# Moving three normalisations off the hand-over between stages of a fused transformer kernel

## The reference, cut to what matters

```
x = x + merged @ w_out
x = x + conv_ffn(rmsnorm(x, ffn_norm_g), w_up, conv_w, conv_b, w_down)      # 22 chunks of 128 columns
x = rmsnorm(x, final_norm_g)                                                # block 1 ends
u_lat = rms_norm(x, norm_g) * (1 + sc_l) + sh_l                             # block 2, 1024 tokens
u_ctx = rms_norm(ctx, norm_g) * (1 + sc_c) + sh_c                           # 256 tokens of context
p_lat = u_lat @ mla_w_in      # query latent (256), key latent (128), rotary part (64), gate (1024)
p_ctx = u_ctx @ mla_w_in[:, kv]
```

## Time and profile before

| | before |
|---|---|
| median of 3 runs (lowest to highest) | 2555.14 us (2554.55 to 2556.97) |
| profiled execution, its own time | 2560.54 us |
| its span | 2558.7 us |
| its mean granted clock of PE | 0.986 |
| PE busy | 2468.8 us, 96% of the span |
| DVE busy | 1513.8 us, 59% |
| ACT busy | 868.5 us, 34% |
| POOL busy | 758.0 us, 30% |
| matmuls L733 (8 chunks of H or H2) | 1070.1 us, x4512 |
| matmuls L1032 (up) on BT, on B | 247.0 us, 190.7 us |
| matmuls L1061 (down) | 239.8 us |

### The profile page before, as it was taken

One profiled execution on the slowest core, in us unless ns is written; L12 is line 12 of the kernel. 1 busy time (PEld: TensorE's weight loads), 2 busy tenths in 40 slices (PEclk: granted clock), 3 DMA queues, 4 the chain that ended last, 5 costly groups with the idle time before them and its releaser, 6 DMA issues.

```text
span 2558.7 us, 33196 instructions
## 1 busy us (share of the span) xinstructions
PE 2468.8 (96%) x12060; PEld 2035.9 (80%) x12060; DVE 1513.8 (59%) x1981; ACT 868.5 (34%) x1290; POOL 758.0 (30%) x442
## 2 busy tenths in 40 slices
PE   7999999999999999999999979999999989899997
PEld 5777787787787888888888868788888878688886
DVE  7856674735557877777411663377777764633454
ACT  4232222223224544445100232156666651222121
POOL 3232232332333555555344412200000003222221
PEclk9999999999999999999999989999999999999999
DMA  5134243421422223233553211100000002111112
GB/s 181 42 115 140 99 149 108 140 74 50 164 107 107 99 107 123 98 113 133 222 194 135 77 41 33 58 1 17 8 8 8 9 9 62 32 40 33 41 41 74
DMA packets 54417, 210.70 MB, mean 82 GB/s; under 512 B 6420, under 2 KB 7700, under 8 KB 49082
## 3 DMA queue, kind: packets, MB, share of 16 engines
q1 hardware_dynamic: 50340, 194.92, 22.0%
q10 hardware_dynamic: 3990, 14.59, 1.6%
HBM read 173.30 MB, written 38.55 MB: 83 GB/s over the span
## 4 chain that ended last, share of the span: by engine, by line
PE 84%; DVE 9%; issue 4%; ACT 1%; DMA 1%; POOL 1%; DVEq 0%; SPq 0%; ACTq 0%; POOLq 0%
PE PS L733 39%; PE PS L1032 16%; PE PS L1061 9%; PE PS L1277 4%; PE PS L1210 3%; PE PS L1216 2%; PE PS L1249 2%; PE PS L891 1%; PE PS L926 1%; DVE cols L2777 1%; PE PS L1200 1%; DVE SC L2327 1%; PE PS L766 1%; PE PS L774 1%; PE PS L1427 1%
## 5 line engine op out<-in xcount | busy, mean ns | idle before, releaser
L733 PE MATMUL PS<-H,w_hl 128*128 128x512 f32 x4512 | 1070.1, 396 | 31.8 <-DVE H L2142 9.4
L733 PEld LDWEIGHTS PS<-H,w_hl 128*128 128x128 f32 x4512 | 847.6, 190 | 231.7 <-issue 33.5
L682 POOL CAST w_hl<-w_raw 128x1024 fp32r<-128x1024 f32 x138 | 155.1, 1124 | 1546.7 <-PE PS L733 1011.8
L684 POOL TENSOR_TENSOR w_hl<-w_raw,w_hl 128x1024 fp32r<-128x1024 f32 x138 | 348.2, 2523 | 11.0
L1032 PE MATMUL PS<-BT,WS 128*128 128x512 f32 x1056 | 247.0, 389 | 0.0
L1061 PE MATMUL PS<-FFD,w_hl 128*128 128x512 f32 x1056 | 239.8, 389 | 0.1
L1032 PEld LDWEIGHTS PS<-BT,WS 128*128 128x128 f32 x1056 | 198.2, 188 | 41.6 <-issue 0.5
L1061 PEld LDWEIGHTS PS<-FFD,w_hl 128*128 128x128 f32 x1056 | 198.1, 188 | 41.6 <-DVEq L2450 0.5
L1032 PE MATMUL PS<-B,WS 128*128 128x512 f32 x792 | 190.7, 395 | 3.6 <-issue 3.6
L1032 PEld LDWEIGHTS PS<-B,WS 128*128 128x128 f32 x792 | 151.1, 191 | 35.7 <-issue 4.0
L689 POOL TENSOR_TENSOR WS<-w_raw,WS 128x512 fp32r<-128x512 f32 x88 | 140.3, 1605 | 73.1 <-ACT WS L1745 72.8
(11 more groups left out here) (341 smaller groups left out, 3005.2 us busy)
## 6 DMA issues: line engine op xcount, KB each, us to landing
w_raw<-in_units SPq DMA_DIRECT2D x186, 512.0 KB, 3.6
AW<-in_ada SPq DMA_DIRECT2D x48, 512.0 KB, 4.2
ff_part<-FFS SPq DMA_DIRECT2D x20, 1024.0 KB, 4.9
FFD<-ff_part SPq DMA_DIRECT2D x20, 1024.0 KB, 5.6
X<-in_x SPq DMA_DIRECT2D x8, 512.0 KB, 8.7
x_part<-SC SPq DMA_DIRECT2D x8, 512.0 KB, 2.6
X<-x_part SPq DMA_DIRECT2D x4, 1024.0 KB, 8.7
out<-X SPq DMA_DIRECT2D x16, 256.0 KB, 2.1
```

What stands on the lines that cost most here:

```text
L682: pool.tensor_copy(hi_part, raw).then_inc(w_hi, 1)
L684: pool.tensor_tensor(lo_part, raw, hi_part.bitcast(F32), ALU.subtract).then_inc(w_split, 1)
L733: mm = pe.matmul(PS[:, out_at + a:out_at + a + m], w(s, wp, w0 + k), src[:, o:o + m], start=(k == 0 and wp == 0 and xp == 0), stop=(k == k ...
```

## The change

Four things change. (1) The query units `cq` run on X * gain, split during `down3` ("rows": ACT `row_hi`, DVE `row_lo`, after each chunk's squares) into H2; the norm's factor r (RS, a copy in SBUF) multiplies their results (`latent_rows`), and the shift enters through `shift_sum`, 16 one-column matmuls for each unit. PE begins `cq` straight after `down3`, with the norm's sum after four chunks, the spread after the first unit. H2 is then rewritten with factor and shift, as before, by `apply_split`, now while the second query unit runs, chunk behind chunk (`h_used`), and `kvpe` waits for it. (2) The context's norm moves forward: ACT loads and squares the context right after the up stage, DVE reduces it before `down0`'s first residual turn; PE sums it within `down0` and spreads it at its end; DVE and ACT write UC between the residuals of `down1` and `down2`. (3) Homes of spilled chunks are dealt anew, and two waits of SP move. (4) In the first up pair the norm's sum goes behind product 3 and its spread behind product 6; ACT takes the first two snapshots before `late_hi`, the weights' high parts 2 and 3 are written earlier, and DVE splits BT2, BT4 and BT3 before it turns to the factor.

```diff
     ("down0", {0: 4, 1: 4, "unit": 4, "xnew": 8}),
+    ("cnorm", {**NORM, "split": 8}),
     ("down1", {2: 4, 3: 4, "unit": 8, "xnew": 8}),
     ("down2", {2: 4, 3: 4, "unit": 8, "xnew": 8}),
-    ("down3", {2: 4, 3: 5, "unit": 8, "xnew": 9, "square": 18}),
-    ("norm3", {2: 2, 3: 1, "norm": 1, "split": 16}),
+    ("down3", {2: 4, 3: 5, "unit": 8, "xnew": 9, "square": 18, "split": 8}),
+    ("norm3", {**NORM, "split": 8}),
...
-    HOMES = [[2, 3, 0, 1], [4, 5, 6, 7, 8, 9], [10, 11, 12, 13, 14, 15], [0, 1, 2, 3, 4, 5]]
+    HOMES = [[2, 3, 0, 1], [4, 5, 8, 9, 10, 11], [6, 7, 0, 1, 2, 3], [8, 9, 10, 11, 14, 15]]
...
                 for half in range(2):
-                    sp.wait_ge(done[half], before("down1", half))
+                    sp.wait_ge(done[half], before("cnorm", half))
+        for half in range(2):
+            sp.wait_ge(done[2 + half], before("down2", 2 + half))
         for k in range(4):
             ff_load(3, k)
             load_until(d0 + 14 + k)
-        for half in range(2):
-            sp.wait_ge(done[2 + half], before("down2", 2 + half))
+        sp.wait_ge(lo, before("down3", "split"))
         for k in range(4, 6):
...
-                if first and n == 1:
+                if first and n == 3:
                     norm_sum(before("norm2", "norm"), before("norm2", 2), early=before("norm2", "square") - 1)
-                elif first and n == 3:
+                elif first and n == 6:
                     norm_spread(before("norm2", "norm"), before("norm2", 3))
...
                             opens = False
             return mm
 
+        def context_sum():
+
+            pe.wait_ge(st_free, 6 + 3 * FFC)
+            take(2, b("cnorm", 2))
+            pe.wait_ge(acc_ready, before("cnorm", "norm") + 1)
+            for j in range(CTX // P):
+                mm = pe.matmul(PS[:, 2048 + j:2049 + j], ACCX[:, j * P:(j + 1) * P], ones[:, 0:1], start=True, stop=True)
+            mm.then_inc(done[2], 1)
+
+        def context_spread():
+
...
         def first_down():
 
             u0 = before("down0", "unit")
@@ -1084,8 +1105,11 @@
                     down_unit(0, s, 1024, w0=ks, opens=False, k0=ks - 1).then_inc(done[1], 1)
                 else:
                     down_unit(0, s, 0).then_inc(done[0], 1)
+                    if i == 2:
+                        context_sum()
                     take(1, i + b("down0", 1))
                     down_unit(0, s, 1024, w0=ks, opens=False).then_inc(done[1], 1)
...
@@ -1113,25 +1137,33 @@
         for n in range(1, len(DOWN)):
             later_down(n)
 
-        norm_sum(before("norm3", "norm"), before("norm3", 2), ((ACC, T), (ACCX, CTX), (ACC2, T)),
-                 early=before("norm3", "square") - 2)
+        def shift_sum(j, s):
+
+            for k in range(KC):
+                for part in range(2):
+                    mm = pe.matmul(PS[:, 2560 - 512 * j:2561 - 512 * j], w(s, part, k).bitcast(F32), modb[:, k:k + 1],
+                                   start=(k == 0 and part == 0), stop=(k == KC - 1 and part == 1))
+            return mm
+
+        u, rows = before("cq", "unit"), before("down3", "split")
+        take(0, b("cq", 0))
+        pe.wait_ge(w_split, u + 1)
+        feature_major(u % 2, H2, KC * T, T, KC, 0, ready=rows, k1=4)
+        norm_sum(before("norm3", "norm"), before("norm3", 2), ((ACC, T), (ACC2, T)), early=before("norm3", "square") - 2)
+        feature_major(u % 2, H2, KC * T, T, KC, 0, ready=rows, opens=False, k0=4)
+        shift_sum(0, u % 2).then_inc(done[0], 1)
         norm_spread(before("norm3", "norm"), before("norm3", 3))
-        spread_context(before("norm3", 2) + 1)
-
-
-        for j in range(2):
-            u = before("cq", "unit") + j
-            take(j, b("cq", j))
-            pe.wait_ge(w_split, u + 1)
-            feature_major(u % 2, H2, KC * T, T, KC, j * 1024,
-                          ready=None if j else before("norm3", "split")).then_inc(done[j], 1)
-
-        pe.wait_ge(lo, before("norm3", "split") + 16)
+        take(1, b("cq", 1))
+        pe.wait_ge(w_split, u + 2)
+        for k in range(KC):
+            feature_major((u + 1) % 2, H2, KC * T, T, KC, 1024, opens=not k, k0=k, k1=k + 1).then_inc(h_used, 1)
+        shift_sum(1, (u + 1) % 2).then_inc(done[1], 1)
+
         for j in range(2):
             u = before("kvpe", "unit") + j
             take(0, b("kvpe", 0) + j)
             pe.wait_ge(w_split, u + 1)
-            feature_major(u % 2, H2, KC * T, T, KC, 0).then_inc(done[0], 1)
+            feature_major(u % 2, H2, KC * T, T, KC, 0, ready=None if j else before("norm3", "split")).then_inc(done[0], 1)
             take(1, b("kvpe", 1) + j)
...
@@ -1717,6 +1749,7 @@
                     act.activation(y[:, k * HALF:(k + 1) * HALF], x[:, part], ACT.Copy, scale=g).then_inc(y_done, 1)
                     if c == KC - 1:
                         act.activation(SQ[:, part], x[:, part], ACT.Square).then_inc(sq_ready, 1)
+                        high_part(0, 2 + half, 0)
                 if c < KC - 1:
...
 
             b_at, c_at, a_at = SUM_AT[q]
-            snap(p, 1, FIRST[q], b_at)
-            high_parts(0, 1)
             if isinstance(p, int) and p == 0:
-                act.wait_ge(lo, before("out1", "split") + operand_at(4, HK - 1) + 1)
-            if spilled:
-                act.wait_ge(ff_out, p * 16 - 16)
-            snap(p, 2, KEEP[q][:, HALF:T], c_at)
-            if isinstance(p, int) and p == 0:
+                snap(p, 5, GATE[:, HALF:T], b_at)
                 phase_norm("norm2")
-                late_hi(2, (T3_SUMS[1], T3_SUMS[3]))
+                high_parts(0, 5)
             else:
+                snap(p, 1, FIRST[q], b_at)
+                high_parts(0, 1)
+                if spilled:
+                    act.wait_ge(ff_out, p * 16 - 16)
+                snap(p, 2, KEEP[q][:, HALF:T], c_at)
                 ff_high(p - 1, 1 - q, kept)
-            high_parts(1, 3)
-            snap(p, 5, GATE[:, HALF:T], b_at)
-            high_parts(3, 5)
...
             act.activation(PROD, CONV, ACT.Gelu, bias=vec[:, bass.ds(p + VEC["conv_b"], 1)]).then_inc(gl_ready, 1)
 
-        high_part(0, 2, 0)
-        high_part(0, 3, 0)
+        act.wait_ge(x_out, 16 * KC)
+        act.wait_ge(sq_ready, before("norm2", "square"))
+        snap(0, 1, FIRST[0], SUM_AT[0][0])
+        snap(0, 2, FIRST[1], SUM_AT[0][1])
         late_hi(0, (T2_SUMS[1], T2_SUMS[3]))
         high_part(0, 4, 0)
         late_hi(1, (T4_SUMS[1], T4_SUMS[3]))
         high_part(0, 5, 0)
         high_part(0, 6, 0)
+        late_hi(2, (T3_SUMS[1], T3_SUMS[3]))
+        act.wait_ge(lo, before("out1", "split") + operand_at(4, HK - 1) + 1)
+        chain(act.activation(KEEP[0][:, HALF:T], FIRST[1], ACT.Copy))
         act.wait_ge(done[2], before("norm2", 2) + 1)
-        act.wait_ge(x_out, 16 * KC)
         up_pair(0, 0, spilled=False)
...
         xts[0] += FFC
 
-        for p in (2, 3):
-            act.wait_ge(done[p], before("down3", p))
+        act.wait_ge(st_prod, PRODUCTS * FFC)
         act.dma_start(CXR[:, :], t_in["ctx"]).then_inc(ctx_in, 16)
         act.wait_ge(ctx_in, 16)
         act.activation(CXS[:, :], CXR[:, :], ACT.Square).then_inc(cxs_ready, 1)
-        residual("down3", gain="final_g")
+        act.wait_ge(ms_ready, before("cnorm", "norm") + 1)
+        act.activation(fstat[:, 8:10], stat[:, 8:10], ACT.Sqrt).then_inc(sd_ready, 1)
+        act.wait_ge(done[3], before("cnorm", 3) + 1)
+        act.activation(RC[:, :], pair(3, CTX), ACT.Copy).then_inc(r1_ready, 1)
+        act.wait_ge(r1_ready, 2)
+        act.sem_inc(free[3], 1)
+        hi_blocks(UC, CTX, KC, lambda c: modb[:, 16 + c:17 + c])
+        residual("down3", gain="final_g", rows=True)
         act.wait_ge(done[3], before("norm3", 3))
         act.dma_start(CST[:, :], t_in["cs"]).then_inc(cs_in, 16)
         act.wait_ge(ms_ready, before("norm3", "norm") + 1)
         act.activation(fstat[:, :], stat[:, :], ACT.Sqrt).then_inc(sd_ready, 1)
-        hi_blocks(H2, T, KC, lambda c: modb[:, c:c + 1])
-        hi_blocks(UC, CTX, KC, lambda c: modb[:, 16 + c:17 + c])
-
-        for j in range(2):
-            act.wait_ge(done[j], before("cq", j) + 1)
-            chain(act.activation(CQR[:, j * T:(j + 1) * T], pair(j), ACT.Copy))
-            act.sem_inc(free[j], 1)
+        act.wait_ge(done[3], before("norm3", 3) + 1)
+        act.activation(RS[:, :], pair(3), ACT.Copy).then_inc(r1_ready, 1)
+
+        def latent_rows(j):
+
+            part = slice(j * T, (j + 1) * T)
+            act.wait_ge(cqr_ready, j + 1)
             if j:
                 act.wait_ge(sq_added, before("cqnorm", "square") + 1)
-            act.activation(SQ, CQR[:, j * T:(j + 1) * T], ACT.Square).then_inc(sq_ready, 1)
+            chain(act.activation(CQR[:, part], CQR[:, part], ACT.Identity, bias=adac[:, j:j + 1]))
+            act.activation(SQ, CQR[:, part], ACT.Square).then_inc(sq_ready, 1)
+
+        for c in range(KC):
+            xts[0] += 1
```

(82 more changed lines are left out.)

57 lines of the change are left out of this document (46 added, 11 removed).

## The result

The changed kernel takes 2573.82 us (median of 4 runs, 2573.06 to 2577.32) against 2556.05 for the kernel before (4 runs, 2554.55 to 2557.14): a ratio of 1.0072, 95% interval 1.006 to 1.0084, or 17.8 us slower. The direction is the forecast's. The size is twice the 8.9 forecast, and 2573.8 lies above the range's top of 2571. Measured again (e11), the same kernel gave 1.0067 (1.0053 to 1.0081). The profiled execution was the slowest of the four (2577.32 us), 3.5 above their median; the one before was 5.4 above its own.

The account below looks back on a forecast made before the run. PE, busy for 96% of the span, was taken as the bound, with DVE the bound at the up stage's entrance. Parts 1 to 3, -7.7 + 12.9 + 3.7 = +8.9 us, took 2555.1 to 2564.0; range about 2555 to 2571.

Parts of the forecast that it names:

- Part 2, the context: Context's norm moved ahead of DVE's first residual turn of down0: +12.9 us, bounds +8.4 to +15.6.
- The stall: At down0, PE stands still 9.9 us for DVE's first turn, behind the context's load, square and reduction.
- Part 3, the entrance: First up pair: product 3 no longer waits, product 5 still needs DVE's eviction; +3.7 us, bounds -1.3 to +7.6.
- The step behind: Next up pair: PE gets ACT's second snapshot after 9.4 us but wants it after 8.2: +1.2 us.
- rival A: Not slower: part 1 pays in full, -13.7, the rest at its mild end; total -4.8, 2550.3 us; chance 0.10.
- Part 1, the query units: Norm3 after down3: PE goes on without a gap, the kvpe unit ends earlier; -7.7 us, bounds -13.7 to -5.7.
- S, the end of the spread: Norm3: the factor's spread ends at 1496.8 us: 19.1 of terms plus 4.4 of low clock after down3.
- DVE's chain: Norm3: DVE's factor application to H2 and work between its chunks end at S + 28.0, deciding by 2 us.
- The last chunks: Norm3: PE's last chunk of kvpe's first unit behind DVE's chain takes 1.4 us, ending at 1526.2.
- Rival B: Near zero: one-column runs cost no clock, part 1 about -12.1; total +4.5, 2559.6 us; chance 0.17.
- C: The context hurts less: part 2 at only +1.0; total -3.0, 2552.1 us; chance 0.05.
- D: All slow: -5.7 + 15.6 + 7.6 = +17.5, 2572.6 us; chance 0.16.

Follow-up runs that it names:

- e11: The changed kernel itself, measured again without any edit: 2574.32 us, 1.0067.
- e2: The changed kernel with the first up pair's old order restored on PE, ACT and DVE: 2568.39 us, 1.0044.
- e1: The changed kernel with DVE reducing the context's squares after down0's second unit's residual turns, not ahead of the first: 2561.22 us, 1.0019.
- e10: The changed kernel, but DVE only waits for the context's squares ahead of down0's first turn and reduces them behind the second unit's turns: 2569.2 us, 1.0046.
- e3: The changed kernel with both the late context reduction of e1 and the old entrance of e2: 2556.42 us, 0.9996.
- e5: As e3, but DVE's rewriting of H2 reads the norm's factor from PSUM, not from its SBUF copy RS: 2551.33 us, 0.998.
- e8: As e1, but DVE's first eviction into GATE precedes BT3's split, and PE spreads the factor behind the second pair's first product: 2557.26 us, 1.0002.
- e9: As e8, with the factor from PSUM as in e5 and ACT's second-pair snapshots ahead of the first pair's Gelu: 2553.67 us, 0.9986.

## Why the prediction was right in direction and short in size

**Part 2, the context: mechanism right, size near.** Forecast +12.9, by the change's trace +12.9, by those of e11 and e2 +14.2; e1 takes back 12.6 (13.6) and leaves 1.5. That the first trace hits the forecast to the tenth is luck. The stall was to be 9.9 and was 10.31 to 10.56. Its terms in the change's trace: a landing of 8.8 us where 7.4 was taken, a square of 1.91, a reduction of 3.59 where 3.88 was taken, and the first turn at 1258.68, 20.0 us into down0, where 1253.1 - 1233.4 = 19.7 was forecast. The landing came near the three loads beside it (median 9.6), not halfway to the quiet one (4.9); ACT was free for it 5.35 us into the stage, against 6.4 taken. The two misses nearly cancel. The low clock behind the stall, taken at 2.0, was 1.7 in the change and 2.8 in e11 (72 matmuls in 18.27 and 19.43, against 16.6 in e1 without a stall). The 4.4 us that the prediction estimated for the landing from the Trainium skill (DMA: Bandwidth & Descriptors, Anatomy of one DMA) come from a fit for transfers that GpSimd issues, and this one is ACT's; the measured 8.8 to 9.3 us (the change, e2, e10, e11) decide.

**Part 3, the entrance: place right, size short.** Forecast +3.7, trace +6.5, runs 4.8 (e1 to e3) and 5.4 or 6.4 (the change to e2), within the bounds given. Two terms of it were short. I kept the eviction where it was; it began 26.2 us after the first product instead of 24.4 before: +1.9. And I took 2.0 of low clock for products 5 and 6; they took 8.11 up to the spread against 5.5 warm: +0.6. The step behind (+1.2) gave +1.35, with the wait for ACT's second snapshot of 0.61 where it was to be. The prediction's bounds are not quite its own sums: its terms give -1.2 and +7.4, where -1.3 and +7.6 stand, and rival A counts +0.5 as this part's mild end. Neither moves the forecast.

**Part 1, the query units: the failed step.** The forecast said -7.7, with bounds -13.7 to -5.7. The change's trace says -0.8, the mean of the seven with this code -2.7, and e3, less the 1.4 us of the down stages, some -2: outside even the cautious bound of -5.7. PE begins without a gap, the clock falls behind the one-column runs, kvpe's first unit waits for DVE's last chunks: the mechanism is the one forecast, and three terms were mis-sized. One of them, DVE's chain, is short by the same amount in all seven traces; the other two come and go with the clock. In the change's trace:

- *S, the end of the spread.* Forecast 23.5 us after down3, measured 1517.58 - 1491.47 = 26.1. Over the full-clock terms (19.1) stand 0.64 of wait for DVE's squares, which I had in time, and 6.4 that I put down to the low clock, where I took 4.4. I counted a loss after a run, but the runs themselves and the spread are slower too: the second 16 records of the sum take 3.58 instead of 1.84, the spread's step 2.77 instead of 1.3. In e5's profile, where the sum ran at nearly full clock, ACT got the spread 1495.04 - 1471.51 = 23.5 us after down3, the forecast's own value. Over the seven traces S lies between 23.6 and 26.2, 25.1 in the mean.
- *DVE's chain: the step that failed each time.* Forecast S + 28.0, measured S + 30.6 (to 1548.19), and 30.4 to 30.6 in the other six. I took 1.6 us for contention added to that of the earlier trace rows, as if a second split by POOL met DVE as today's does. But the change also turns the factor from PSUM into SBUF, so each multiplication now has two SBUF operands. I priced the copy into RS (1.0, right) and put what reading it costs at nothing. e5 shows that cost: with the factor back in PSUM the chain is S + 27.3.
- *The last chunks.* I took 1.4 us of PE behind DVE's last low part. It was 1551.28 - 1548.19 = 3.1, because the last 12 matmuls began at half clock after their wait (4.61, against 3.06 in e5). Behind the same wait of 2.5 us they took 3.1 in e2, e8, e10 and e11, and the term was 1.5 there, as forecast: what the clock does at this place is chance, as far as the traces show.

2.6 + 2.6 + 1.7 = 6.9 us, the distance from -7.7 to -0.8. In the mean of the seven traces it is 1.6 + 2.6 + 0.8 = 5.0. In DVE's timeline of the change the contended rows are:

```profile
1518.79 4.93 DVE L2191 SCALAR_TENSOR_TENSOR SC<-X,fac,RS 128x1024 f32<-128x1024 f32 x2 [13.35 <-ACT RS L1902]
...
1534.07 1.94 DVE L2191 SCALAR_TENSOR_TENSOR SC<-X,fac,RS 128x1024 f32<-128x1024 f32 x1
1535.93 3.43 DVE L2204 SCALAR_TENSOR_TENSOR H<-SC,modb,H 128x1024 fp32r<-128x1024 f32 x1
```

Against 2.47 for two and 1.28 for one they lose 2.5 + 0.7 + 2.15 = 5.3 us; e5 gets 3.2 of it back. The trace of before had the sign. Beside one operation of POOL, a multiplication with the factor in PSUM keeps its 1.28 us, while the low part behind it, with two SBUF operands, takes 2.10:

```profile
1494.83 3.24 POOL L684 TENSOR_TENSOR w_hl<-w_raw,w_hl 128x1024 fp32r<-128x1024 f32 x1
```

```profile
1495.87 1.28 DVE L2129 SCALAR_TENSOR_TENSOR SC<-X,fac,PS 128x1024 f32<-128x1024 f32 x1
```

**The cases.** Rival B (one-column runs cost no clock) is refuted in the change's own rows: 1.00, then 0.50 within the first shift sum, without a gap. With it falls, for this kernel, what the prediction drew from the Trainium skill (TensorE: Matmul & The Clock Gate, HAM oscillation), that it is idle gaps which bring the half clock. A and C fall with e3 and e1. D's sum (+17.5) comes closest to the result, but by another way: it had part 1 at -5.7 and the worst of the other two. The range failed because its upper end combined the bounds of parts 2 and 3 with a part 1 that always gained at least 5.7, and because it stopped at 2571, below D's own 2572.6. No case said "part 1 gives next to nothing", though my own two chains ended within 2 us of each other and each had an unpriced term.

## What to carry to other kernels

Work that fills a gap on the bound engine gives the gap's time only if it runs at the gap-free rate: runs of one-column matmuls cost their own time (7.8 us here), and the half clock on what followed. When a change swaps an operand's place (PSUM for SBUF), price every instruction that reads it beside POOL, not only the copy. And when a serial piece (load, square, reduction) is moved ahead of another engine's first turn, its whole length counts; putting the last link behind that turn, and with it the wait for the chain, as in e1, took the stall away whole.

## What the hardware showed that I had not expected

- **Half clock without any gap, and not each time alike.** With the same PE order up to there, the sum's second 16 records took anything from 1.95 us (e5, e8, e10) to 3.58 (the change), and norm3's stretch 55.7 (e10) to 59.9 us (e3) with the same code there. A single profile can't price an edit there to better than some 4 us; the intervals of 11 runs are about 2.3 us to either side. Behind the 32 records of a shift sum the half clock came in every trace that has them in a row (4 matmuls of the spread until the next group in 2.06 to 2.78 us, where 1.3 is warm), and in neither of the two that break them up (1.4).
- **Both sides of the contention pay.** POOL's operation of 2.42 us beside the pair with a PSUM factor (e5) is 3.25 beside the one with the SBUF factor (e3), while DVE's pair goes from 2.47 to 4.93.
- **A stage without stalls repeats to the hundredth.** From the third up pair to down0 the kernel before takes 1233.42 - 852.62 = 380.80 us, e3 1232.37 - 851.57 = 380.80, e9 1231.61 - 850.81 = 380.80, and so do all the 13 traces. What differs between them lies elsewhere: ahead of the third pair, at the down stages' stall, in norm3 and behind it.
- **One load, two landing times.** The context's 1 MB took 4.9 us in its old quiet place and 8.8 to 9.3 in its new one (the change, e2, e10, e11), where the core's other loads were under way. That these are the reason was not tested.
